# A two-block network on one core: mixture of experts in F32R passes with weights split on chip and fetched during routing, transposed router product, ranks by prefix sums, one delta-rule output

## The reference, cut to what matters

```python
# token mixer: the two directions of the delta rule are added, then normalised and gated
o = gdn_chunked(q, k, v, g_f, beta_f) + rev(gdn_chunked(rev(q), rev(k), rev(v), rev(g_b), rev(beta_b)))
o_b = from_heads(rms_norm_2(o, gdn_norm_w)) * silu(dz)
x = x + (sigmoid(m_a) * o_a + sigmoid(m_b) * o_b) @ w_out
# mixture of experts: 1024 tokens of width 1024, 4 groups of 8 experts, 2 experts each
group_idx = argmax(t @ w_group)
top_p, top_i = top_k(softmax((t @ w_router)[that group]), 2)
# the 2048 assignments are sorted by expert and worked on in blocks of 128 rows
hid = silu(xs @ w_gate[e]) * (xs @ w_up[e])     # 1024 -> 256
y = hid @ w_down[e]                             # 256 -> 1024
out = rms_norm_2(x + sum of the two weighted y, norm_f_w)
```

## Time and profile before

| what | value |
|---|---|
| median of 3 runs | 4293.95 us (4292.23 to 4297.89) |
| the profiled execution's own time | 4307.94 us |
| its span, first to last instruction | 4306.1 us |
| TensorE busy | 3561.2 us, 83% of the span |
| VectorE, ScalarE, GpSimd busy | 1697.1, 1108.2, 1094.8 us |
| mean granted TensorE clock | 0.902 of full speed |
| moved by DMA | 541.5 MB |
| `dl_` / `jo_` / `rt_` stages | 3043 to 3522 / 3522 to 3675 / 3675 to 3766 us |
| `ex_` / `ov_` / `cb_` stages | 3766 to 4201 / 4201 to 4238 / 4238 to 4306 us |

### The profile page before, as it was taken

One profiled execution on the slowest core, in us unless ns is written; L12 is line 12 of the kernel. 1 busy time (PEld: TensorE's weight loads), 2 busy tenths in 40 slices (PEclk: granted clock), 3 DMA queues, 4 the chain that ended last, 5 costly groups with the idle time before them and its releaser, 6 DMA issues. The chain is left out here.

```text
span 4306.1 us, 58360 instructions
## 1 busy us (share of the span) xinstructions
PE 3561.2 (83%) x23778; PEld 2725.6 (63%) x23778; DVE 1697.1 (39%) x2371; ACT 1108.2 (26%) x2069; POOL 1094.8 (25%) x775
## 2 busy tenths in 40 slices
PE   3599688798669999978999999887599969589991
PEld 0599544487544555456888888665588857466660
DVE  4401344462236666543355111354345547111113
ACT  0111122442322333331253111352233224011111
POOL 0000122320032444411242454101444423110002
PEclk7799788799888999998999999998899989599995
DMA  7222200442374231043233221226444446299965
GB/s 270 96 80 77 76 5 10 152 152 81 95 245 91 50 72 44 13 149 108 76 93 93 75 82 46 59 64 189 127 115 113 108 149 236 90 366 333 320 223 205
DMA packets 346451, 541.50 MB, mean 126 GB/s; under 512 B 60927, under 2 KB 230655, under 8 KB 343777
## 3 DMA queue, kind: packets, MB, share of 16 engines
q1 hardware_dynamic: 325470, 479.00, 35.6%
q10 hardware_dynamic: 13184, 33.56, 2.4%
q0 software_dynamic: 7568, 25.70, 1.6%
HBM read 398.48 MB, written 139.71 MB: 125 GB/s over the span
## 5 line engine op out<-in xcount | busy, mean ns | idle before, releaser
L2329 PE MATMUL mx_ps_p<-mx_wh,h 128*128 128x512 f32 x1280 | 397.3, 392 | 0.0
L455 PE MATMUL in_ps_p<-in_wh,h 128*128 128x352 f32 x1280 | 306.4, 322 | 11.1 <-DVE in_wl L468 11.1
L2329 PEld LDWEIGHTS mx_ps_p<-mx_wh,h 128*128 128x128 f32 x1280 | 242.1, 189 | 50.2
L1889 ACT ACTIVATE la_pt<-la_ps_s 128x1024 f32<-128x1024 f32 x160 | 163.7, 1023 | 400.6 <-PE la_ps_s L1851 400.6
L1851 PE MATMUL la_ps_s<-la_q,la_k 104*128 104x512 f32 x960 | 254.5, 401 | 2.5 <-DVE la_q L1931 2.5
L3789 PE MATMUL ex_ps_g<-ex_wgu,ex_xt 128*128 128x256 f32 x1024 | 233.6, 387 | 27.1 <-ACT ex_xt L3823 13.4
L1806 POOL TENSOR_TENSOR la_accp<-la_accp,la_pt 128x1024 f32<-128x1024 f32 x80 | 195.1, 2438 | 229.5 <-ACT la_pt L1889 229.5
L2329 PE MATMUL mx_ps_p<-mx_wl,h 128*128 128x512 f32 x640 | 250.3, 391 | 0.0
L2322 PE MATMUL mx_ps_p<-h,mx_wh 128*128 128x512 f32 x768 | 238.6, 392 | 0.0
L3789 PEld LDWEIGHTS ex_ps_g<-ex_wgu,ex_xt 128*128 128x128 f32 x1024 | 195.1, 193 | 60.5 <-DVE ex_xt L3840 19.3
L455 PEld LDWEIGHTS in_ps_p<-in_wh,h 128*128 128x128 f32 x1280 | 222.3, 188 | 11.5 <-DVE in_wl L468 11.5
(11 more groups left out here) (605 smaller groups left out, 7260.5 us busy)
## 6 DMA issues: line engine op xcount, KB each, us to landing
ex_wgu<-in_moe_w_gate_dram SPq DMA_DIRECT2D x32, 1024.0 KB, 8.1
ex_wgu<-in_moe_w_up_dram SPq DMA_DIRECT2D x32, 1024.0 KB, 10.6
ex_wd<-in_moe_w_down_dram SPq DMA_DIRECT2D x32, 1024.0 KB, 8.5
ada_w<-in_w_ada_dram SPq DMA_DIRECT2D x12, 2048.0 KB, 18.6
mx_w<-in_w_in_dram SPq DMA_DIRECT2D x16, 1024.0 KB, 5.5
mx_w<-in_w_in_dram SPq DMA_DIRECT2D x32, 512.0 KB, 5.0
dl_row<-rows SPq DMA_DIRECT2D x32, 512.0 KB, 4.8
yb<-ex_y SPq DMA_DIRECT2D x32, 512.0 KB, 6.3
```

The costliest lines, as they stand in the source:

```text
L455: mm = te.matmul(ps[n % NB][:, 0:cw], a, b, start=k == 0 and n_ == 0, stop=k == kt - 1 and n_ == 2)
L1889: act.activation(pt[t % NPT][:], ps[t % 2][:], ACT.Exp, scale=scale).then_inc(*act_s.did(flat(o)))
L2329: mm = te.matmul(ps[bank[n] // 2][:, bank[n] % 2, :], a, b, start=k == 0 and m == 0, stop=k == KT - 1 and m == 2)
```

## The change

- **Delta rule.** For chunks 0 to 7 `oo` goes to `out[0]` for both directions. From chunk 8 on, the other direction has already written the same tokens: SyncE loads them (`part`, into `early`), GpSimd adds them to `oo` (`oa0`, `oa1`) and SyncE stores the sum to `out[1]` (`whole`). ScalarE's wait before it overwrites `oo` is now for that store. `join_out` loads one tensor where it loaded two, and `fb` is gone.
- **Clearing.** The 7.5 MB of `yb` are cleared in `gdn_loop`, on SyncE's queue, ahead of chunk 1's loads.
- **Router.** The 36 router columns are stationary and 512 tokens move. The two halves of the tokens go to PSUM partitions 0 and 64. ScalarE copies twice, 8 transposes bring the logits back, VectorE copies twice.
- **Ranks.** VectorE sums `both` over the tiles (`cum`, 8 steps). TensorE then needs one matmul by `bef`, one by `ones`, and one for the counts.
- **Weights ahead.** During `routing` SyncE loads experts 0 and 1, and expert 2 once the router product has released `h3t`, whose memory it takes.
- **Experts** (`experts_stream`, written out for all 32). Three landing buffers. ScalarE copies the high parts (`gh0` to `gh3`, `dh`), VectorE subtracts the low ones (`gl0` to `gl3`, `dl`); rows and hidden values are split in the same way. Gate and up are one product of 512 columns. The 16 scatters now open this stage, one DMA loads the token numbers of all 32 experts, and GpSimd gathers one expert after the other. `ov` and `combine` are as before.

```diff
 def gdn_loop(...):
-        for nm, i in (("kl", n1), ("kn0", n1), ("kn1", n1), ("qd0", n1), ("qd1", n1), ("W1", n3), ("W2", n3), ("D1", n3), ("D2", n3), ("Di", n3)):
+        for nm, i in (("oa1", c - 1), ("kl", n1), ("kn0", n1), ("kn1", n1), ("qd0", n1), ("qd1", n1), ("W1", n3), ("W2", n3), ("oa0", c), ("D1", n3), ("D2", n3), ("Di", n3)):
...
+                def whole(c, g):
+                    sp.wait_ge(*pool.at(f"oa{g}_{c}"))
+                    for d in both:
+                        t0 = chunk(c, d) * C2
+                        sp.dma_start(out[1][t0:t0 + C2, g * BANK:(g + 1) * BANK], oo[g][half[d], :, :].rearrange("p h n -> p (h n)")).then_inc(o_out[g], 16)
...
                 for c in range(NC):
+                    if c == 1:
+                        sp.wait_ge(clr, 1)
+                        sp.dma_start(to_clear.rearrange("(b p) n -> p b n", p=P), zrow[:].rearrange("p (b n) -> p b n", b=1).to_broadcast([P, OVER, D])).then_inc(cleared, 16)
...
+                    for g in both:
+                        if c - 2 >= NC // 2:
+                            whole(c - 2, g)
+                        if c - 1 >= NC // 2:
+                            part(c - 1, g)
...
+                        op = gp.tensor_tensor(oo[g][:], oo[g][:], early[g][:], ALU.add)
 def routing(...):
-                sp.dma_start(yb[NE * P:SLOTS, :].rearrange("(b p) n -> p b n", p=P),
-                             zrow[:].rearrange("p (b n) -> p b n", b=1).to_broadcast([P, OVER, D])).then_inc(yz, 16)
                 sp.dma_start(row_tok.rearrange("(p n) a -> p (n a)", p=P), zero[:]).then_inc(zin, 16)
+                ahead(sp, False)
+                sp.wait_ge(mm_s, 1)
+                ahead(sp, True)
...
-                for i in range(nt):
-                    if i >= 2:
-                        te.wait_ge(ev, i - 1)
-                    for k in range(KT):
-                        mm = te.matmul(ps[i % 2][:, 0:NL], h_t[:, k, i * P:(i + 1) * P], wl[:, k, :], start=k == 0, stop=k == KT - 1)
+                for k in range(KT):
+                    for j in range(2):
+                        mm = te.matmul(ps[sides[j], :], wl[:, k, :], h_t[:, k, j * BANK:(j + 1) * BANK], start=k == 0, stop=k == KT - 1)
...
+                te.matmul(pr[:], bef[:], every(both[:]), start=True, stop=False)
+                te.wait_ge(a, 4)
+                te.matmul(pr[:], ones[:], every(cum[:, 0:nt, :]), start=False, stop=True)
+                te.matmul(pc[:], ones[:], cum[:, nt, :], start=True, stop=True).then_inc(mm_s, 1)
+def experts_stream(nc, ident, h, row_tok, dest, tok, w_gate, w_up, w_down, yb, land, xs, gu_in, d_in):
+    for s in range(-2, NE + 1):
+        for o, names in ((pe_order, (("gu", s), ("xt", s + 2), ("y", s - 1), ("ht", s))),
+                         (act_order, (("sg", s), ("xh", s + 2), ("gh0", s + 2), ("ya", s - 1), ("gh1", s + 2), ("hh", s), ("gh2", s + 2), ("gh3", s + 2), ("dh", s + 1))),
+                         (dve_order, (("hd", s), ("xl", s + 2), ("gl0", s + 2), ("yv", s - 1), ("gl1", s + 2), ("hl", s), ("gl2", s + 2), ("gl3", s + 2), ("dl", s + 1)))):
...
+                        sp.dma_start(yb[(s - 1) * P:s * P, :], y[(s - 1) % 2][:]).then_inc(y_st[(s - 1) % 2], 16)
+                    gate_up(s + 2 + NL)
+                    down(s + 1 + NL)
...
+                        act.wait_ge(sc_s, 16 * 2 * (S // P))
+                        act.dma_start(idx[:], row_tok[0:NE * P, :].rearrange("(e p) a -> p (e a)", p=P), allow_slow_non_contiguous=True).then_inc(i_in, 16)
...
+                        for k in range(KT):
+                            for n, (a, b) in enumerate(passes((xh[s][:, k, :], xl[s][:, k, :]), (wh[s][:, k, :, :], wl[s][:, k, :, :]))):
+                                mm = te.matmul(pg[s][:].rearrange("p g n -> p (g n)"), a, b.rearrange("p g n -> p (g n)"), start=k == 0 and n == 0, stop=k == KT - 1 and n == 2)
```

More of the change, by code:

```diff
@@ L2950, in _, with gdn_loop @@
                 ve.tensor_copy(rt[:, BANK:], pr[:, 1, :]).then_inc(rowd, 1)
-def gdn_loop(nc, ident, qk, c2, rows, cols, de, kq, tri, out):
+def gdn_loop(nc, ident, qk, c2, rows, cols, de, kq, tri, out, to_clear):
     NC, H, C2, W = S // GC, DH, GC, DH * GC
@@ L2996, in gdn_loop @@
         state = st.sb("S", [P, 2, H, P])
+        early = [st.sb(f"early{g}", [P, 4, P]) for g in both]
+        e_in = [st.sem(f"e_in{g}") for g in both]
         K = [st.ps(f"K{g}", [P, 4, P]) for g in both]
@@ L3030, in rows_for, with part @@
                                          row_of(rows[0, d, chunk(c, d), :, :, :].rearrange("q h n -> (q h n)"), C2)).then_inc(r1_in[c % 2], 16)
+                def part(c, g):
+                    sp.wait_ge(o_out[g], 32 * (NC - c))
+                    after(sp, pool, f"oa{g}_{c - 1}")
+                    for d in both:
+                        t0 = chunk(c, d) * C2
+                        sp.dma_start(early[g][half[d], :, :].rearrange("p h n -> p (h n)"), out[0][t0:t0 + C2, g * BANK:(g + 1) * BANK]).then_inc(e_in[g], 16)
+                def whole(c, g):
+                    sp.wait_ge(*pool.at(f"oa{g}_{c}"))
+                    for d in both:
+                        t0 = chunk(c, d) * C2
+                        sp.dma_start(out[1][t0:t0 + C2, g * BANK:(g + 1) * BANK], oo[g][half[d], :, :].rearrange("p h n -> p (h n)")).then_inc(o_out[g], 16)
                 rows_for(0)
@@ L3046, in _ @@
                         sp.dma_start(v[half[d], :, :].rearrange("p h n -> p (h n)"), c2[t0:t0 + C2, :]).then_inc(v_in, 16)
+                    for g in both:
[3 more added lines that the diff above has]
+                            part(c - 1, g)
+                for g in both:
+                    whole(NC - 2, g)
+                    part(NC - 1, g)
+                for g in both:
+                    whole(NC - 1, g)
                 for g in both:
                     sp.wait_ge(o_out[g], 32 * NC)
+                sp.wait_ge(cleared, 16)
             @block.gpsimd
             def _(gp):
+                gp.memset(zrow[:], 0.0).then_inc(clr, 1)
                 gp.wait_ge(par, 16 * (4 + NC))
@@ L3514, in _, with routing @@
                         ve.scalar_tensor_tensor(ht[s][:], xt[s][:], sx[s][:], g_t[:], ALU.mult, ALU.mult).then_inc(*dve.did(o))
-def routing(nc, h_t, w_group, w_router, before, row_tok, yb, dest, wts, n_over, over_e):
+def routing(nc, ident, h_t, w_group, w_router, before, row_tok, tok, dest, wts, n_over, over_e, ahead):
     nt = S // P
@@ L3617, in _ @@
                 ve.wait_ge(cst, 8)
-                ve.wait_ge(ev, nt)
+                ve.wait_ge(mm_s, 2)
+                for j in range(2):
+                    step(ve.tensor_copy(lg[:, j * nt // 2:(j + 1) * nt // 2, :], pl[j][:]))
                 gl = lg[:, :, 0:NGR]
@@ L3645, in _ @@
                 ve.sem_inc(a, 1)
-                ve.wait_ge(ev, nt + 2)
+                for i in range(nt):
+                    step(TT(cum[:, i + 1, :], cum[:, i, :], both[:, i, :], ALU.add))
+                ve.sem_inc(a, 1)
+                ve.wait_ge(ev, 4)
                 step(ve.tensor_reduce(gs[:], gx[:], AX.X, ALU.add))
```

261 lines of the change are left out of this document (216 added, 45 removed).

## The result

The changed kernel takes 4193.3 us (median of 4 runs, 4188.5 to 4199.3), the kernel before 4295.9 (4 runs): ratio 0.975, 95% interval 0.972 to 0.979. On another chip (e11) the ratio was 0.973, 0.971 to 0.976. Forecast were 4191 us, in a range of 4158 to 4238.

What follows compares the result with a forecast made beforehand. TensorE was taken as the bound in the steady experts, 191.0 of 210 us busy. Terms -79 - 14 - 16 + 9.5 - 5 + 1.5 = -103 from the 4294 median gave 4191 us, range 4158 to 4238.

Steps and rivals of the forecast that it cites:

- Experts: Experts' stage: bound moves from TensorE to the DMA queues at 383 GB/s; 336 us against 415.3, -79.
- The sign: Experts' stage: TensorE 85 to 90% busy, waiting for splits that wait for landing, with transfers at 370 to 390 GB/s.
- transfers fall short: Rival for the experts' stage: only 350 GB/s holds, stage 364 us, total 4219; chance 0.20.
- TensorE stays the bound: Rival for the experts' stage: transfers hold 400 GB/s and more, stage 317 us, total 4172; chance 0.13.
- Slower rival: Experts: VectorE's subtractions contend with GpSimd's gathers by a factor 2.2, step 17.6 us, total 4433; chance 0.04.
- Router product: Routing: two column groups overlap, product taken as 10 us; with transposes and copies 13.9 instead of 27.9, -14.
- Ranks: Routing, from `both` to the counts: 3.3 us instead of 19.2 through sums and fewer matmuls, -16.
- Start: Experts' start, `dest` to first product: 46 us instead of 40.5, plus 4 for delayed scatters, +9.5.
- The scatters' +4: Experts' start: some scatters wait for the rest of a VectorE subtraction, +4 us, between 0 and 8.
- The rival without overlap: Router product: its two halves do not overlap, +17 us; part of the failed-start rival, total 4213, chance 0.12.
- Delta loop and join: Delta loop +1.5 for the sum before the last store; join -5 from gating without `fb` and shorter loads.
- the clear: Delta loop: clearing 7.9 MB, 20 us at 383 GB/s, ends before chunk 1's keys are needed, 0 to +3.

Runs made afterwards that it cites:

- e11: The changed kernel itself, unaltered, run on another chip beside two other variants: 4191.1 us, ratio 0.973 to the kernel before.
- e2: Changed kernel with the gathers of experts 2 to 31 left out: ratio 0.968 to the kernel before, experts' stage 307.0 us.
- e4: Changed kernel with gate and up weights read in pieces of 8 KB instead of 1 KB, transposes strided to match: 4170.6 us, ratio 0.968.
- e3: Changed kernel without gathers of experts 2 to 31 and stores of experts 0 to 29, slots cleared earlier: one run, 4185.5 us, experts' stage 300.9.
- e8: Changed kernel with both halves of the router product in the same column group, in two banks: ratio 0.978 to the kernel before.
- e6: Changed kernel with the splits of experts 0 and 1 started only after the sixteen scatters: ratio 0.973 to the kernel before.
- e7: Changed kernel with the first three experts' weights loaded at the start of the experts' stage, not during routing: 4222.5 us, ratio 0.980.
- e12: Changed kernel with 8 KB pieces for gate and up and the results stored from ScalarE's queue: 4184.3 us, ratio 0.972.
- e1: Changed kernel with the experts' results stored from ScalarE's queue instead of SyncE's: ratio 0.974 to the kernel before, experts' stage 339.6 us.
- e5: Changed kernel with gathers skipping slots that hold no token, weights still in 1 KB pieces: ratio 0.974 to the kernel before.
- e9: Changed kernel with empty slots skipped in the gathers and tokens spread over the partitions: 4204.7 us, ratio 0.976.
- e10: Changed kernel with 8 KB pieces for gate and up, empty slots skipped and tokens spread over the partitions: 4176.5 us, ratio 0.970.

## Why the prediction was right, point by point

- **Experts** (-79 predicted, -74.4 measured). Right, and for the reason given: the bound moved from TensorE to the queues, shown by e2 and e4, at 382 GB/s where 383 had been taken. The sign was another one than forecast: the engines wait for stores, not for splits that wait for weights. The parts came out as 16 + 301 + 24 against 15 + 299 + 22. The engines' step of 9.5 was 9.34 in the steady part of e3 (9.25 over the stage). What the prediction did not ask is what 383 depends on. It took "the nearest row with transfers queued", and the pieces were the same there, so the number held; e4 shows that it belongs to the pieces. The Trainium skill, "DMA: Bandwidth & Descriptors", section "Where 436 GB/s comes from", has some 358 GB/s per core between HBM and SBUF; the 382 held for 270 us here and the 419 in e4 disagree with it.
- **Rival "transfers fall short"**: did not occur; with stores and gathers all the time the rate stayed at 382. **Rival "TensorE stays the bound"**: its stage of 317 would have needed less work in the queues; e4 comes to 314 that way. **Slower rival**: subtractions of 1.22 us, not 2.5. GpSimd pays instead, in the sixteen scatters and in gathers of 1.6 us on average (0.96 in the kernel before), and has time for it.
- **Router product** (-14, -16.2). Overlap as assumed (e8). The product was 9.2 where 10 was taken, and the transposes' 1.5 was 0.45. The rival without overlap was priced too high: +17, with all 28 us at half clock, where e8 costs 7, since its clock rose within the first 5 us as well.
- **Ranks** (-16, -15.6). Right.
- **Start** (+9.5, +6.2). The scatters' +4 was +4.5, shown by e6 and e7. Its sum was a little pessimistic: from the first gather's issue to the product 10.7 us pass where 8.6 + 2 + 1 + 1.3 + 2 = 15 were taken; the gather itself, from its start to the first transpose, took 4.7, not 8.6. The earlier trace rows do not show that figure; in the same trace the gather at 3770.7, beside loads of weights, takes 8.7 to its transpose. The Trainium skill, "SBUF — State Buffer", section "Who interferes with whom", infers that `tensor_tensor` leaves descriptor generation alone, and that does not hold here: up to 2.00 us for a scatter beside subtractions, 0.96 without; and 0.94 for all 23 gathers of e12 from 3790 to 4020, which start while VectorE is idle.
- **Delta loop and join** (+1.5 and -5 predicted; together -3.8). The sum is near partly by luck: the loop gained where nothing was forecast. Timeline of ScalarE in the loop before; its two issues of stores stand between `oo` and `M`:

```profile
3382.21 0.60 ACT L3205 ACTIVATE dl_oo<-dl_ps_K 128x512 f32<-128x512 f32 x1 [4.82 <-PE dl_ps_SP L3135]
3385.03 0.60 ACT L3197 ACTIVATE dl_MX<-dl_ps_TX 128x512 f32<-128x512 f32 x1 [2.23 <-PE dl_ps_TX L3172]
3385.04 1.10 ACTq L3186 DMA_DIRECT2D gdn<-dl_oo  x2
3386.19 0.60 ACT L3194 ACTIVATE dl_M<-dl_ps_Pb 128x512 f32<-128x512 f32 x1 [0.56 <-PE dl_ps_K L3121]
...
3392.20 0.60 ACT L3205 ACTIVATE dl_oo<-dl_ps_K 128x512 f32<-128x512 f32 x1 [1.03 <-PE dl_ps_SP L3135]
```

and the same place after, where these chunks are stored by SyncE:

```profile
3375.90 0.60 ACT L3244 ACTIVATE dl_oo<-dl_ps_K 128x512 f32<-128x512 f32 x1 [4.82 <-PE dl_ps_SP L3172]
3378.73 0.60 ACT L3236 ACTIVATE dl_MX<-dl_ps_TX 128x512 f32<-128x512 f32 x1 [2.23 <-PE dl_ps_TX L3209]
3379.22 0.59 ACT L3233 ACTIVATE dl_M<-dl_ps_Pb 128x512 f32<-128x512 f32 x1
...
3385.22 0.60 ACT L3244 ACTIVATE dl_oo<-dl_ps_K 128x512 f32<-128x512 f32 x1 [1.03 <-PE dl_ps_SP L3172]
```

`M` follows at once, the second output stands 9.32 behind the first instead of 9.99, and from the ninth chunk on a chunk takes 27.4 instead of 28.1. The same trace has the comparison: its first eight chunks, still stored from ScalarE, stand 28.1 apart. From first to last `oo` the loop takes 417.1 us before and 412.2 after. I had counted what the sums add to GpSimd and SyncE, and not what leaves ScalarE, whose issues stood on the chain. Against it, the first `oo` comes 4.9 us later after the point of comparison; in eleven other traces with this loop and the same clear it comes 0.8 to 6.0 later (2.1 in e11). Whether that is the clear, which was given 0 to 3, is not shown: in e3, with the threefold clear, the first `oo` comes 0.6 us earlier than before, and its delay of some 30 us follows only between the first two outputs. So this trace's -3.8 for the stage is one of a spread from -3.0 to -7.8 over these twelve traces, all against the one trace of the kernel before. What follows the last `oo` holds the two effects that were forecast, the sum that stands before the last store (+1.5) and the join (-5): to the join's first transpose 31.6 became 29.7, from there to the router product 128.5 became 126.6, -3.8 where -3.5 had been predicted.

No kernel was made that has the delta and join part, or the ranks, alone; these terms rest on the stage lengths of the traces.

## What to carry to other kernels

When a stage moves from an engine to the queues, take the rate from a row whose pieces are those of the new stage, and ask what it would be with longer pieces: here over three quarters of the packets had 1 KB, and reading neighbouring rows into one partition, with a matching stride in the transpose, was worth as much as a quarter of the whole change. The wait that a profile shows in such a stage (here for the stores) may be only where the shortage comes to light: move it, and if the step stays, it was probably not the bound, unless the move itself put in another wait, as in e1. Look at single steps and not only at their mean: a stage that starts with a lead runs at the engines' step until it is used up. Price also what a moved instruction frees on the engine that it leaves, and never put a wait for another engine ahead of work on an in-order engine for the sake of a transfer.

## What was not expected of the hardware

- Most packets of 1 KB: 382 GB/s; most of 4 KB and more: 419, the same bytes (e4).
- A gather of which half the rows are skipped moved half the bytes (13.1 to 6.3 MB) and freed nothing (e5, e9, e10).
- A load of 16 KB in single words on one queue took 18.5 us beside large loads on another, 4.2 with few (e7).
- Two DMA issues on ScalarE, 1.10 us together, delayed the next activation by 0.67 us, and each chunk by as much.
- 16 float32 products of 512 columns with 36 columns of weights (32 instructions): 9.2 us in two column groups, 16.2 in one (e8).
- Indirect transfers of GpSimd that start beside an idle VectorE take 0.94 to 0.97 us (the first of a series up to 1.2), most that start during a subtraction of two SBUF operands 1.7 and more (e6, e7, e12).
